# Early products between the rows of the modulation, P6 begun in a bank of its own, and x's turns in two banks

## The reference

```
mod = silu(c) @ ada_w + ada_b
shift, scale, gate = split(mod, 3)
h = rms_norm(x, norm_pre) * (1 + scale) + shift
q, k, v, z = slices of h @ diff_w_in          # 2048 x 8192
o = softmax(mask(q1 k1)) v - lam * softmax(mask(q2 k2)) v, per head
o = rms_norm(o, subln) * (1 - lambda_init) * silu(z)
y = o @ diff_w_out
out = x + gate * rms_norm(y, norm_post)
```

## Time and profile before

| what | value |
|---|---|
| median of 3 runs | 1915.87 us (1914.35 to 1917.17) |
| the profiled execution, its own time | 1914.27 us |
| its span, first to last instruction | 1912.5 us |
| mean granted TensorE clock | 0.989 |
| PE busy | 1865.4 us, 98% of the span |
| DVE, ACT, POOL busy | 72%, 42%, 42% |
| DMA | 247 GB/s in the mean |

### The profile page before, as it was taken

One profiled execution on the slowest core, in us unless ns is written; L12 is line 12 of the kernel. 1 busy time (PEld: TensorE's weight loads), 2 busy tenths in 40 slices (PEclk: granted clock), 3 DMA queues, 4 the chain that ended last, 5 costly groups with the idle time before them and its releaser, 6 DMA issues.

```text
span 1912.5 us, 26374 instructions
## 1 busy us (share of the span) xinstructions
PE 1865.4 (98%) x9072; PEld 1544.5 (81%) x9072; DVE 1384.3 (72%) x2026; ACT 812.5 (42%) x1520; POOL 795.6 (42%) x844
## 2 busy tenths in 40 slices
PE   4899999999999999999999999999999999999998
PEld 1578888888878888888888888888888888888886
DVE  2687888786665546787877777878778776569468
ACT  4633333333444433444443444444444445546452
POOL 2066565565654523344343434434443422016023
PEclk6999999999999999999999999999999999999999
DMA  9798898886675778786877778686777678657777
GB/s 354 244 303 277 272 302 277 286 284 242 225 253 176 295 277 267 224 247 196 255 224 229 234 215 251 197 253 211 231 240 220 213 230 290 204 189 256 263 234 261
DMA packets 393905, 473.17 MB, mean 247 GB/s; under 512 B 22598, under 2 KB 268460, under 8 KB 391084
## 3 DMA queue, kind: packets, MB, share of 16 engines
q1 hardware_dynamic: 393488, 471.43, 76.1%
q10 hardware_dynamic: 284, 0.05, 0.0%
HBM read 323.54 MB, written 147.86 MB: 246 GB/s over the span
## 4 chain that ended last, share of the span: by engine, by line
PE 91%; DMA 2%; DVE 2%; SPq 2%; ACT 1%; POOL 1%; issue 1%; DVEq 0%; POOLq 0%; ACTq 0%
PE ps L1701 29%; PE ps L1702 29%; PE ps L1703 29%; PE ps L1832 2%; PE ps L1806 1%; PE ps L1851 1%; ACT blk L1027 1%; SPq L585 1%; SPq L453 1%; DMA x2s<-in_x_dram 1%; ACT h L1003 0%; DVE ring L1254 0%; DMA raw<-in_diff_w_in_dram 0%; PE ps L1670 0%; DVE blk L1301 0%
## 5 line engine op out<-in xcount | busy, mean ns | idle before, releaser
L1701 PE MATMUL ps<-blk,ring 128*128 128x512 f32 x1524 | 604.3, 396 | 2.7 <-ACT cc L1014 1.3
L1703 PE MATMUL ps<-blk,ring 128*128 128x512 f32 x1524 | 596.0, 391 | 0.0
L1702 PE MATMUL ps<-blk,ring 128*128 128x512 f32 x1524 | 595.6, 391 | 0.0
L1701 PEld LDWEIGHTS ps<-blk,ring 128*128 128x128 f32 x1524 | 286.9, 188 | 63.1 <-issue 5.4
L1703 PEld LDWEIGHTS ps<-blk,ring 128*128 128x128 f32 x1524 | 286.6, 188 | 60.7
L1702 PEld LDWEIGHTS ps<-blk,ring 128*128 128x128 f32 x1524 | 287.0, 188 | 56.1
L1254 DVE TENSOR_TENSOR ring<-sums,ring 128x512 fp32r<-128x512 f32 x256 | 230.4, 900 | 95.8 <-ACT ring L969 94.1
L809 POOL TENSOR_TENSOR sums<-raw 128x512 f32<-128x512 f32 x128 | 194.5, 1520 | 246.5 <-DVE ring L1254 148.4
L969 ACT ACTIVATE ring<-sums 128x512 fp32r<-128x512 f32 x256 | 160.6, 628 | 178.0 <-PE ps L1703 177.9
L1254 DVE TENSOR_TENSOR ring<-raw,ring 128x512 fp32r<-128x512 f32 x192 | 183.1, 954 | 57.1 <-ACT ring L969 56.5
L1533 DVE TENSOR_TENSOR ub<-ubf,ub 128x1024 fp32r<-128x1024 f32 x113 | 154.7, 1404 | 62.4 <-ACT ub L1129 61.5
(11 more groups left out here) (154 smaller groups left out, 3191.5 us busy)
## 6 DMA issues: line engine op xcount, KB each, us to landing
raw<-in_diff_w_in_dram SPq DMA_DIRECT2D x64, 1024.0 KB, 7.7
d_dr<-cc SPq DMA_DIRECT2D x124, 256.0 KB, 3.2
cc<-d_dr SPq DMA_DIRECT2D x124, 256.0 KB, 4.0
ubf<-s_dr SPq DMA_DIRECT2D x113, 256.0 KB, 5.2
ada<-in_ada_w_dram SPq DMA_DIRECT2D x88, 256.0 KB, 7.4
tb<-in_diff_w_out_dram SPq DMA_DIRECT2D x32, 512.0 KB, 5.3
t_dr<-tb SPq DMA_DIRECT2D x32, 512.0 KB, 5.1
ada<-in_ada_w_dram SPq DMA_DIRECT2D x32, 512.0 KB
```

Source lines behind the costliest of these rows:

```text
L1701: MM(dst, a_hi, b_hi, start=start, stop=False, skip_group_check=True)
L1702: MM(dst, a_hi, b_lo, start=False, stop=False, skip_group_check=True)
L1703: return MM(dst, a_lo, b_hi, start=False, stop=stop, skip_group_check=True)
```

## The change

Four things are changed together. P6 becomes an early product too, and for that it gets a bank of its own (`VX`), in which P7 and P4 of the first group then go on; since P6 is to be added to P1, each k-step of P1 is done twice, once into P1's bank and once into `VX`. The early products move from behind `mod_turn` to between the fifth and the sixth row of the group. x's turns use two banks instead of three, so a turn waits for the scaling two turns back; two turns stand ahead of the early products, two behind `mod_turn` (in the first group all four). And ACT's copy of the next group's row bank moves ahead of the last rounding of the group.

```diff
-    X_BANK = (5, 6, 7)
+    X_BANK = (5, 6)
-    EARLY_PRODUCTS = (0, 1, 3)
+    EARLY_PRODUCTS = (0, 1, 2, 3)
...
         def bank_of(i, pi):
             if i == 0 and pi in (P5, P3):
                 return 1
+            if i == 0 and pi in (P6, P7, P4):
+                return VX
             return Y if pi in (P2, P5, P3) else i % 2
...
+            def copy_row(j):
+
+                act.wait_ge(*taken(8 * j + 7))
+                if j:
+                    act.wait_ge(mod_turned, j)
+                A(mod_row[:, :], ps[:, ROW_BANK], ACT.Copy).then_inc(mod_row_ok, 1)
+
+            copy_row(0)
             for j in range(4):
-                act.wait_ge(*taken(8 * j + 7))
-                A(mod_row[:, :], ps[:, ROW_BANK], ACT.Copy).then_inc(mod_row_ok, 1)
...
                 for y in LOWS[2:]:
+                    if j < 3 and y == LOWS[-1]:
+                        copy_row(j + 1)
                     high_h(y)
...
-                    if y >= 3:
-                        pe.wait_ge(h_ev, y - 2)
+                    if y >= 2:
+                        pe.wait_ge(h_ev, y - 1)
...
-                    three(ps[:, bank_of(0, pi)], ring[:, pi, 0, j], ring[:, pi, 1, j],
-                          slotA[pi][:, 0, j], slotA[pi][:, 1, j], j == 0, False)
+                    for bank in (bank_of(0, pi), VX)[:1 + (pi == P1)]:
+                        three(ps[:, bank], ring[:, pi, 0, j], ring[:, pi, 1, j],
+                              slotA[pi][:, 0, j], slotA[pi][:, 1, j], j == 0 and pi != P6, False)

             for ch in range(4):
                 for r in range(8):
                     if r == 5 and ch:
-                        for q in range(3):
+                        for q in range(len(X_BANK)):
                             x_turn(4 * ch + q)
+                        begin(ch - 1)
                     ada_rows(8 * ch + r)
-                if ch == 0:
-                    for q in range(3):
-                        x_turn(q)
                 mod_turn(ch)
-                if ch:
-                    begin(ch - 1)
-                x_turn(4 * ch + 3)
+                for q in range(len(X_BANK) if ch else 0, 4):
+                    x_turn(4 * ch + q)
...
-                elif pi == P6:
+                elif pi == P6 and i:
                     pe.wait_ge(*read_out(i, P1))
...
+                    if n == 0:
+                        three(ps[:, VX], ring[:, n % RING, 0, j], ring[:, n % RING, 1, j], at_[:, 0, j], at_[:, 1, j],
+                              False, False)
```

More of the change, by code:

```diff
@@ L1002, in modulate @@
                 act.wait_ge(xT_mm, y + 1)
-                A(h32[:, q // 2, half * HALF:(half + 1) * HALF], ps[:, X_BANK[y % 3] if js < 4 else VX], ACT.Identity,
+                A(h32[:, q // 2, half * HALF:(half + 1) * HALF], ps[:, X_BANK[y % 2] if js < 4 else VX], ACT.Identity,
                   scale=mod[:, KT + k:KT + k + 1], bias=mod[:, k:k + 1]).then_inc(h_ev, 1)
@@ L1669, in x_turn @@
                     c = k * P if js < 4 else k % (KP // 2) * P
-                    i = TR(ps[:, X_BANK[y % 3] if js < 4 else VX, t * P:(t + 1) * P], tile[:, c:c + P], ident[:, :])
+                    i = TR(ps[:, X_BANK[y % 2] if js < 4 else VX, t * P:(t + 1) * P], tile[:, c:c + P], ident[:, :])
                 i.then_inc(xT_mm, 1)
```

## The result

The changed kernel takes 1924.63 us (median of 6 runs, 1922.04 to 1926.8), the kernel before beside it 1916.30. The ratio is 1.0044, with a 95% interval of 1.0034 to 1.0054: by it the change is 8.4 us slower (6.5 to 10.3). The forecast was 1924.9, or +9.0. The profiled execution took 1923.70 (span 1921.9), 9.4 more than that of before.

What follows compares the result with a forecast made beforehand. The prediction took the ACT and DVE chain to set group time before, TensorE's rows after. Its terms, +6.7 for the groups, -0.3 behind them and +2.6 for the clock, gave +9.0: 1924.9 us, range 1919 to 1928.5.

Steps and rivals of the forecast that it cites:

- Who bounds a group: In each group, ACT's row-bank copy would wait for TensorE's rows, starting at 11.70 instead of 9.38; group 13.9 us, not 11.57.
- the prediction's last paragraph: Signs for the next profile; the forecast would be wrong if the copy ran straight behind the fourth rounding.
- The first turns: First group: with mod_turn ahead of x's turns, the first ACT scaling would come 2.0 us earlier, at 45.05.
- The first group: From the first group's first scaling to the second's: rows at half clock until 50.7, second group's first scaling at 60.6.
- The clock: TensorE's waits ahead of the later groups' turns and the steady stretch: two of three clock falls, 1.3 us each, +2.6.
- the rival with a fall in every stretch at full price: Three clock falls in TensorE's waits cost 5.1 us; total +11.5, 1927.4 us; chance 0.20.
- the likeliest: The whole kernel: the main forecast with two clock falls, +9.0, 1924.9 us; chance 0.42.
- Behind m12: From the fourth group's first scaling to the steady stretch: 0.3 us gained, as P6's matmuls leave the last turn's way.
- the rival that TensorE bounds this stretch: Behind the fourth group's first scaling, P6's early matmuls would pay: 1.4 less, +7.6, 1923.5 us; chance 0.08.
- the 1.37 us: TensorE time saved later, before the steady stretch, by what it called three matmuls less; counted as nothing.
- The loads: SP's row loads: the last would land at 80, needed only at 84.3, so the delay costs nothing.
- The other side: Rows through in time, moved copy fills ACT's gap, groups shrink by up to 1.9; total -2.4, 1913.5 us; chance 0.07.

Runs made afterwards that it cites:

- the filler's run: Changed kernel plus unneeded row matmuls, four behind mod_turn and two between the last two turns of a group; 1924.57 us, ratio 1.0048.
- the move alone: Kernel before with only the nine early products moved between the rows, three banks kept; 1920.49 us, ratio 1.0029.
- the one with filler: Kernel before with only the nine early products moved between the rows, plus six unneeded row matmuls behind mod_turn; 1919.32 us, ratio 1.0018.

## Why the prediction was right, point by point

*Who bounds a group.* Right. The copy waits for the rows, and the rows come after TensorE's own sum. (It runs behind the sixth rounding; the prediction's last paragraph says the fourth.) In the second group of the changed kernel, from m4 at 59.66: the closing turn waits for the second scaling and starts at 2.16 (forecast 2.13); two turns 0.85 (0.97); the fifteen matmuls 3.62 (67.57 to 71.19; forecast 3.52); the last rows 1.88; the copy to m8 2.21 (2.18). The stretch between, from the closing turn to the next two turns, took 4.90 us (61.82 to 66.72) instead of 3.20, and that is the clock.

*The first turns.* Right: m0 at 45.21, forecast 45.05; alone they give some 2 us (0.9988), as the run with them shows.

*The first group.* The mechanism right, the size off by 1.1: m0 to m4 14.45 us, forecast 15.55. I had let the clock rise where it rose before; here it rose earlier and the five rows took 2.74. That was luck: where TensorE's work ahead of these rows is the same, they took up to 2 us longer (see the last section).

*The clock.* The term that was mis-sized, +2.6 for two falls of 1.3. In the profiled execution all three waits had a fall: 15.67 - 13.9 = 1.8 in the second group, 16.39 - 13.9 = 2.5 in the third, and behind m12 19.56 - 18.82 = 0.7, if the filler's run is taken as the one without a fall. That is 5.0, and 2.4 too little in the sum. The fall in the third group cost more than the 1.7 that I had taken as the most for one fall: from the closing turn to the next two turns it is 5.63 us (77.49 to 83.12) instead of 3.20. The first group (1.1 too much) took part of it back; so +10.3 at the next product stands against +9.0. By its falls the profiled execution is the rival with a fall in every stretch at full price (5.1); that the time came out near the likeliest, to 0.3 us in the median, is in part two errors of opposite sign, and so in part luck. The Trainium skill, "TensorE: Matmul & The Clock Gate", section "HAM oscillation — how this bites in real kernels", has it, of waits for DMA, that every burst behind a wait pays again. The changed kernel and the move alone, with waits for ACT, agree with it in both groups (0.89 and 0.79, 0.87 and 0.87). Where the wait was filled, the move alone no longer paid (0.87 became 1.00); the changed kernel still paid in its second group (0.89) and not in its third (0.79 became 1.00).

*Behind m12.* Right that the nine matmuls of P6 done early gain nothing there, but the 0.3 that was taken off is not theirs. The stretches from m12 to the next product, of the kernel before, of the one with the copy and the first turns alone, and of the changed kernel with filler:

```profile
81.75:100.97 19.22, 17.82 (x70) 12.86 (x69) 15.71 (x21) 11.90 (x21) 6.60 (x5) 0.92 0.29 93
...
80.30:99.11 18.81, 16.51 (x69) 11.80 (x68) 15.66 (x21) 11.80 (x21) 6.52 (x4) 1.00 0.32 102
...
91.61:110.43 18.82, 15.47 (x71) 10.04 (x64) 15.68 (x21) 11.67 (x21) 6.94 (x5) 1.00 0.28 96
```

The kernel before has a fall of the clock of its own here (0.92; the nine matmuls of 81.50 to 84.90 ran at 0.51). Where the clock holds, the stretch is 18.81 without P6 early and 18.82 with it. In all three the next product still waits for DVE's eviction (0.16, 0.17 and 0.16 us), as in the changed kernel (0.16, at 111.28). So the 0.4 us between 19.22 and 18.82 are the clock's, the changed kernel with its own fall is 0.3 longer here and not 0.3 shorter, and the rival that TensorE bounds this stretch has fallen. (P6's nine out and three in are six matmuls less, not three; the 1.37 us are those of six.)

*The loads.* Right: behind m0 no row waits for a landing in the changed kernel, and where the groups are made faster the loads bound at m12 = 80.30 (forecast 79.7).

*The other side.* Its mechanism is real, and it needs the early products elsewhere: the copy moved alone saves a microsecond a group, because there the copy can start 8.1 behind the first scaling (67.81, m4 at 59.70). It is not the 1.9 of the prediction: the rows are not through earlier, and from the copy to m8 it is 2.46 us (70.27) instead of 2.18. In the changed kernel the copy starts at 13.5. What I did not see: behind mod_turn the early products fill the wait, and in two of the three groups of the kernel before the clock held there (not in the third, 0.51); the move alone lost both together, as its run and the one with filler show.

## What to carry to other kernels

Before moving work into another engine's idle stretch, add up what the engine does in program order up to the point that somebody waits for: here 1.3 us of room stood in front of the copy (66.68 to 68.00), and the move put 3.5 us of matmuls and a longer wait into it. Work that stood in a wait of TensorE was worth its place twice here: it cost little there, and with it gone the granted clock fell from 1.00 to 0.87 in the groups of the move alone. When several edits are made together, run each alone: the first turns gained clearly, the moved copy at the edge of the noise, both together no more than the first turns, since the loads let only one of the gains through, and the other two edits, P6 early and the moved early products, gained nothing.

## What the runs showed of the hardware that I had not expected

The clock's rise in the first group differs between executions of the same work, by more than the effects under study. Ahead of the five rows of the second `ch`, TensorE's work is the same in the changed kernel, with P6 left out, with `begin` put back and with the filler in the changed kernel; the rows took 2.74, 2.74, 4.76 and 4.84 us there. It is the same in the kernel before, with only the early products moved, with these and filler, and with the copy alone: 3.59, 2.74, 4.44 and 5.03 us. The two runs with the first turns moved had 3.24 and 3.73. Each is one profiled execution, and nothing in the kernels' work ahead of the rows explains the order. So one profile's first group can't be compared with another's to better than some 2 us, and comparisons were made from m4 on. In three of these profiles (4.76, 4.84 and 5.03) the granted clock reads 1.00 over rows that take nearly twice as long as the 2.67 us of a group at full clock; that they ran at the lower clock is read from their durations, and the column alone would have misled.

The filler's row matmuls write a single partition each, and with six of them in the wait two groups ran at 1.00 that had run at 0.87. In the changed kernel four and two of them were not enough in one group of two (0.89 and 1.00).
